# Up and down projections of the first layer in one program per engine

## The chip, the cores and the metric

The kernel runs on one core of a Trainium2 chip, in float32. The metric is the device time of one execution in microseconds (us): 2348.28 us is the median of three runs of the kernel before, which lie between 2337.39 and 2351.69 us. In the rows PE is TensorE's matmul side and PEld its weight loads, DVE is VectorE, ACT is ScalarE, POOL is GpSimd and SP is SyncE. A float32 matmul shows as two records in the trace.

## The reference

Two layers of a diffusion transformer act on 512 image tokens and, in the first layer, on 256 context tokens as well (width 1024). The change lies where the first layer's feed-forward part is computed and where the second layer begins:

```python
def conv_ffn(h, w_up, conv_w, w_down):            # d_ff = 2816
    a, g = jnp.split(dwconv(h @ w_up, conv_w), 2, axis=-1)   # depthwise, 3 taps over tokens
    return (jax.nn.silu(g) * a) @ w_down
...
        x = x + mx[:, :, 2] * rmsnorm(ox, norm_g[l, 1])
        hx = modulate(rmsnorm(x, norm_g[l, 2]), mx[:, :, 3], mx[:, :, 4])
        x = x + mx[:, :, 5] * rmsnorm(conv_ffn(hx, ffn_w_up[l], ffn_conv[l], ffn_w_down[l]), norm_g[l, 3])
        # the same for the context rows z in the first layer
...
    mx = (sc @ w_mod[l] + b_mod[l])               # of the next layer, l = 1
```

## The kernel before

The program is a row of stages. Each stage is a Block, in which every engine has its own list of instructions; at the end of a Block all engines meet before the next Block starts. The stages that matter here are `mix_and_up` (L1933: output projection of the mixer, then the up projection) and `down_and_project` (L2739: the down projection, then the second layer's input projections). Both are called from `layer_ab` (L3491, L3492). The second layer has the two in one Block already (`up_down_and_store`, L2963).

**Weights.** All weights come through a ring of four slots (`c.ring`). SP issues the loads in the order in which they are used; each waits until the products that read the slot's earlier content are done. In the up stage (`c.issue`, L182) the loads run up to four ahead of the stage's end, so the first four loads of the down projection (`down0x`) are issued there: two when the last column pair but one is done, two when the last is. The later ones are issued in the down stage (`c.stream`, L193): the two loads of part q wait for the products of part q-2.

**Up projection** (`mix_and_up_programs`, L1449). The 22 pairs of gate and value columns are numbered n = 0 to 21 (`FT` = 22). From n = 1 on, each pair is one Strassen step: seven products `p1, p2, p6, p5, p7, p3, p4`, each of four matmuls, on quarters of weights and tokens and on sums of quarters, which DVE makes (`join_weights(n)`, four additions, L1851 to L1856). The results are gathered from the banks by one ACT copy (L1708) and seven DVE additions (`add_up`, L1860, semaphore `whole`). In DVE's list pair n does this in order: `join_weights(n + 1)`, `convolve_pair(n - 1, 0)` and `convolve_pair(n - 1, 1)` (two taps each, L387 and L391), the additions of pair n, and among them `multiply(n - 1)` (L1829, semaphore `done`), after ACT's silu (L1678). After the last pair DVE calls `between()`, which does nothing in `mix_and_up`, then the convolutions of pair 21 and `multiply(21)`. The hidden rows, 22 tiles of 768 tokens, lie in the arena.

**Down projection** (`DownPairs`, L2367, and `FirstDownPairs`, L2514). The image rows are done in 8 steps, again of Strassen form. A step has three parts over the hidden rows k: `PARTS = ((0, 4), (4, 8), (8, 11))`; each part has the seven products in the order above, and the 21 products of a step accumulate in seven banks. DVE makes the sums of rows (`join_rows(group, part)`, L2562 to L2567) once for each group of four steps and the sums of weights (`join(q)`, L2429 to L2434) for each part. PE reads the weights for p1 and p2 as they are, waits for two sums before p6 and for four before p7. The third part reads hidden rows 8 to 10 and 19 to 21.

**Work beside it.** The second layer's modulation is computed in the down stage. POOL first issues five small loads of the filter network (`net.load`, L3564 to L3567; they go to `c.small`) and then the loads of `w_mod` (`load_side`, L2605, L2610), 512 KB each, two buffers in turn at the end of the arena. PE multiplies each loaded piece in its own list of instructions, between products of the down projection:

```python
    def behind_product(self, pe, s, n):                  # n: product 0 to 20 of step s
        if s < 4 and n % 5 == 0 and n:
            self.side_product(pe, 4 * s + n // 5 - 1)
    ...
    def side_product(self, pe, q):
        pe.wait_ge(self.mod_in[q % 2], 16 * (q // 2 + 1))   # piece q has landed
```

Products are counted through the parts, so n = 5 is p3 of part 0, n = 10 is p5 of part 1, n = 15 is p2 of part 2. ACT starts the down stage by issuing 24 small loads (L284, L295) and then keeps p1 of each step (`keep_first`, L2483).

`mix_and_up_programs` returns the lists of the engines and two waits, `gathered` (all additions of the up projection done) and `complete` (`done` at 22, so the last `multiply` is done).

Of the kernel before, what the change touches and what calls it, by code (L numbers as in the profile page):

```python
# [22 lines left out]
D = 1024  # L23
# [371 lines left out]
def outc(c):  # L395

    return c.arena[:, 0:KT * N_ALL].rearrange("p (k t) -> p k t", k=KT)
# [1051 lines left out]
def mix_and_up_programs(c, l, z, name, src, sem):  # L1449
# [261 lines left out]
        middle(FT - 1, 1)  # L1711
        gate(FT - 1)

    def vector(dve, between):
        v = nc.vector
        link = chain(dve, dve_chain)
        per = 2 if z else 1
# [177 lines left out]
        for n in range(begun, FT):  # L1895
            i = n - begun
            gate_rows, value_rows = ([fast.raw(n, half)[:, at:at + fast.half] for at in (0, fast.half)] for half in range(2))
            if n + 1 < FT:
                join_weights(n + 1)
            if i:  # L1900
                convolve_pair(n - 1, 0)
                convolve_pair(n - 1, 1)
            dve.wait_ge(copied, i + 1)
            add_up(i, gate_rows[1], gate_rows[0], "p6")
            add_up(i, gate_rows[0], gate_rows[0], "p2")
            multiply(n - 1)
            dve.wait_ge(whole, 7 * i + 1)
            add_up(i, value_rows[0], gate_rows[1], "p7")
            dve.wait_ge(whole, 7 * i + 3)
            add_up(i, value_rows[1], value_rows[0], "p5")  # L1910
            add_up(i, gate_rows[1], gate_rows[1], "p5")
            dve.wait_ge(whole, 7 * i + 5)
            add_up(i, gate_rows[1], gate_rows[1], "p3")
            add_up(i, value_rows[0], value_rows[0], "p4")
            join_hidden(n - 1)
# [12 lines left out]
            pe.wait_ge(hidden_joined, 4 * (FT // 2))  # L1928

    return sync, tensor, scalar, vector, gathered, complete  # L1930


def mix_and_up(c, l, z, name, src):  # L1933


    st, sem = stage(c)
    sync, tensor, scalar, vector, _, _ = mix_and_up_programs(c, l, z, name, src, sem)
    with st, c.nc.Block() as block:  # L1938
        @block.sync
        def _(sp):  # L1940
            sync(sp)

        @block.tensor
        def _(pe):
            tensor(pe)

        @block.scalar
        def _(act):
            scalar(act)

        @block.vector
        def _(dve):
            vector(dve, lambda: None)


class FastPairs:
# [557 lines left out]
class FirstDownPairs(DownPairs):  # L2514
# [8 lines left out]
    def __init__(self, c, sem, rows, side):  # L2523
        DownPairs.__init__(self, c, sem, rows)
        self.side, self.hidden = side, ffn_hidden(c)[0]
        self.mod_in = [sem("mod_in_even"), sem("mod_in_odd")]
        self.mod_used, self.mod_drained, self.rows_in, self.rows_joined, self.weighed = (
            sem(n) for n in ("mod_used", "mod_drained", "rows_in", "rows_joined", "mod_weighed"))
        late, gate, spare = c.ht[:, 4 * D:6 * D], c.gates[:, 0].rearrange("p u d -> p (u d)"), c.arena[:, FT * N_ALL:]
        whole = lambda ap: [ap[:, 128 * lo:128 * hi] for lo, hi in self.PARTS]  # L2530
        self.first_sums = (whole(late), whole(gate), [spare[:, 0:512], late[:, 1408:1920], gate[:, 1408:1792]])

    def weight_sums(self, q):
        slots = [(self.lo + 2 * q + h) % RING * SLOT + 1024 for h in range(2)]
# [201 lines left out]
                between(dve, n)  # L2736


def down_and_project(c):  # L2739

# [5 lines left out]
    spread = Spread(c, 1, sem)  # L2748
    pairs = FirstDownPairs(c, sem, rows, spread.m)
    down = Down(c, sem, rows, spread.m, pairs)  # L2750
    n_pairs, n_rope = 8, 2
    last_raw = c.ht[:, 4 * D:5 * D].rearrange("p (b t) -> p b t", b=2)
    row = lambda n: q[:, n, :] if n < 4 else u[:, n - 4, :]
# [11 lines left out]
    with st, nc.Block() as block:  # L2765
# [2 lines left out]

        @block.sync
        def _(sp):  # L2770
            for name in ("down0x", "down0", "swa_q", "hy_in", "swa_k", "swa_v"):
                c.stream(sp, name, 0 if name == "swa_v" else RING)

        @block.gpsimd
        def _(pool):
            net.load(pool)
            pairs.load_side(pool)

        @block.tensor
        def _(pe):  # L2780
            pe.wait_ge(c.tables_back, 32)
            for s in range(pairs.STEPS):
                pairs.step(pe, s)
            pe.wait_ge(pairs.copied, pairs.STEPS)
            pe.wait_ge(pairs.whole, 7 * pairs.STEPS)
            pe.wait_ge(pairs.mod_drained, 2)
# [48 lines left out]

        @block.scalar
        def _(act):
            spread.m.load_biases(act, pairs.rows_in)
            spread.m.load_gains(act, pairs.rows_in)
            for s in range(pairs.STEPS):  # L2840
                pairs.keep_first(act, s)
                pairs.square(act, s)

            def unit(n):
                if n % 2 == 0:
                    down.keep_act(act, n)
                if n:
                    down.square(act, n - 1)

            for q in range(n_units):  # L2850
                unit(q)
                if q == 1:
                    for i in range(TX):
                        rows.branch_root(act, i)
                if q in (3, 4):
                    for i in range(2 * (q - 3), 2 * (q - 3) + 2):
                        rows.norm_root(act, i)
                if 5 <= q < 5 + TX:
                    rows.modulate_act(act, q - 5, turn_banks)
            down.square(act, n_units - 1)  # L2860
            for i in range(TX, TT):
                rows.branch_root(act, i)
            rows.norm_root(act, TX)

            def others(act, i):
                if i == 0:
                    rows.norm_root(act, TX + 1)
                    rows.modulate_act(act, TX, late_banks)
                if i == 1:
                    rows.modulate_act(act, TX + 1, late_banks)  # L2870
                if i == 7:
                    net.sine(act, 0)
                if i in (4, 5):
                    act.wait_ge(rows.added, TT)
                    spread.keep_gate_act(act, i - 4, i - 4, 0, gate_banks)

            fast.scalar(act, others)
            net.sine(act, 1)
            swa_k.scalar(act)
            for t in range(0, TT, 2):  # L2880
                act.wait_ge(v_product, t + 1)
                nc.scalar.activation(v_[:, t, :], c.ps[:, (0, 2, 4, 5)[t % 4], 0:128], ACT.Copy).then_inc(v_act, 1)

        @block.vector
        def _(dve):
            dve.wait_ge(c.tables_back, 32)
            parts = pairs.n_parts
            for s in range(pairs.STEPS):
                group, first = s // pairs.PER_GROUP, s % pairs.PER_GROUP == 0
                if s == 0:  # L2890
                    pairs.join_rows(dve, 0, 0)
                    pairs.join(dve, 0)
                for part in range(1, parts):
                    if first:
                        pairs.join_rows(dve, group, part)
                    pairs.join(dve, parts * s + part)
                    if s >= 4:
                        pairs.weigh_behind(dve, s, part)
# [585 lines left out]
def layer_ab(c):  # L3484
# [3 lines left out]
    chunk_products(c)  # L3488
    delta_rule(c)
    gdn_output(c)  # L3490
    mix_and_up(c, 0, N_Z, "ab_out", outc(c))  # L3491
    down_and_project(c)  # L3492


def cd_buffers(c):
# [655 lines left out]
```

## Time and profile before

| | |
|---|---|
| median of three runs | 2348.28 us (2337.39 to 2351.69) |
| profiled execution, its time | 2345.86 us |
| profiled execution, its span from first to last instruction | 2344.1 us |
| PE busy | 2150.0 us, 92% of the span |
| DVE busy | 1497.9 us, 64% |
| mean granted clock of TensorE | 0.966 |
| up projection's last products, end | about 1218.0 us from the span's start |
| first product of the down projection | 1225.65 us |

In the timelines the first number is the start in us from the span's start, the second the length; "[idle before <-releaser]" is the engine's idle time ahead of the piece and what ended it. "xN" counts records. Pieces are merged, so a piece can hold short waits. In the table of stretches PEclk is the granted clock, 1.00 for 2.4 GHz and 0.50 for 1.2 GHz.

### The profile page before, as it was taken

What the parts mean: (1) busy time and instruction counts of PE and PEld (TensorE: products, weight loads), DVE (VectorE), ACT (ScalarE), POOL (GpSimd) and SP (SyncE); (2) the same over time, 40 slices, a digit from 0 to 9 for tenths busy, and PEclk for the clock granted to TensorE, in tenths of its full rate; (3) what the DMA queues carried; (4) which work ended last, traced back from release to release, by engine and by line L of the source; (5) the groups of instructions that cost most, each with busy time, mean ns of one, the idle gap of its engine ahead of it and who ended that gap; (6) DMA issues with size and microseconds to landing.
All of it is one profiled execution on the core that took longest, in us unless ns stands there. A gap on an engine that the chain in (4) does not pass through costs nothing. (4 is left out here: it accounts for less than half of the span.)

```text
span 2344.1 us, 38947 instructions
## 1 busy us (share of the span) xinstructions
PE 2150.0 (92%) x16226; PEld 1633.5 (70%) x16226; DVE 1497.9 (64%) x2822; ACT 539.1 (23%) x1187; POOL 248.8 (11%) x335
## 2 busy tenths in 40 slices
PE   5999989969997999999989989897888799999998
PEld 3566655558886755555558889785454588888998
DVE  4534856567775666665665656674676756778754
ACT  3103732431213421111110012111451032111111
POOL 2000100037760000000000111000210000000000
PEclk8999989989999999999999999998898899999999
DMA  8450002100004112122217678332000213323454
GB/s 311 146 196 19 1 19 54 36 2 4 4 4 145 37 53 55 54 54 67 59 56 245 219 221 247 112 90 68 1 1 19 72 37 90 86 80 87 141 167 143
DMA packets 235633, 205.09 MB, mean 87 GB/s; under 512 B 6771, under 2 KB 219458, under 8 KB 235266
## 3 DMA queue, kind: packets, MB, share of 16 engines
q1 hardware_dynamic: 222050, 157.07, 22.6%
q0 software_dynamic: 12416, 42.32, 5.4%
q10 hardware_dynamic: 992, 3.21, 0.4%
q8 instruction: 129, 2.11, 0.4%
q14 instruction: 46, 0.38, 0.1%
HBM read 200.48 MB, written 2.10 MB: 86 GB/s over the span
## 5 line engine op out<-in xcount | busy, mean ns | idle before, releaser
L1599 PE MATMUL banks<-mem 128*128 128x384 f32 (+1 forms) x2296 | 622.1, 433 | 0.0
L1599 PEld LDWEIGHTS banks<-mem 128*128 128x128 f32 x2296 | 434.4, 189 | 187.2
L2453 PE MATMUL banks<-mem 128*128 128x128 f32 x2464 | 285.5, 277 | 18.1 <-PEq L1938 7.7
L2453 PEld LDWEIGHTS banks<-mem 128*128 128x128 f32 x2464 | 279.3, 192 | 29.5 <-issue 23.5
L2013 PE MATMUL banks<-mem 128*128 128x256 f32 (+1 forms) x672 | 180.0, 424 | 9.4 <-ACT mem L3385 5.1
L2013 PEld LDWEIGHTS banks<-mem 128*128 128x128 f32 x672 | 128.4, 193 | 60.7 <-issue 21.3
L1860 DVE TENSOR_TENSOR mem<-mem,banks 128x384 f32<-128x384 f32 (+1 forms) x287 | 131.1, 487 | 39.4 <-PE banks L1599 36.7
L694 PE MATMUL banks<-mem 128*128 128x384 f32 x448 | 146.4, 485 | 2.1 <-PEq L440 1.4
L996 PE MATMUL banks<-mem 64*64 64x64 f32 x3840 | 127.7, 220 | 18.5 <-DVE mem L1272 11.4
L996 PEld LDWEIGHTS banks<-mem 64*64 64x64 f32 x3840 | 120.1, 136 | 28.7 <-DVE mem L1272 13.7
L1524 PE MATMUL banks<-mem 128*128 128x256 f32 x560 | 127.2, 388 | 11.0 <-PEq L1388 8.8
L1524 PEld LDWEIGHTS banks<-mem 128*128 128x128 f32 x560 | 108.5, 195 | 28.0 <-issue 11.8
L1851 DVE TENSOR_TENSOR mem<-mem 128x512 f32<-128x512 f32 x41 | 28.4, 694 | 154.4 <-DMA mem<-in_ffn_w_up 154.4
L694 PEld LDWEIGHTS banks<-mem 128*128 128x128 f32 x448 | 84.6, 189 | 60.5 <-issue 1.6
L1678 ACT ACTIVATE mem<-mem 128x768 f32<-128x768 f32 (+1 forms) x44 | 32.5, 739 | 346.5 <-DVE mem L391 346.5
L391 DVE SCALAR_TENSOR_TENSOR mem<-mem 128x511 f32<-128x511 f32 (+1 forms) x160 | 100.9, 659 | 3.8
L387 DVE SCALAR_TENSOR_TENSOR mem<-mem 128x511 f32<-128x511 f32 (+1 forms) x160 | 100.6, 658 | 1.2 <-ACT mem L2054 1.1
L1687 ACT ACTIVATE mem<-mem 128x768 f32<-128x768 f32 (+1 forms) x82 | 66.1, 829 | 146.5 <-DVE mem L1860 146.3
L2340 PE MATMUL banks<-mem 128*128 128x128 f32 x704 | 82.5, 278 | 2.6 <-DVE mem L2186 2.4
L2340 PEld LDWEIGHTS banks<-mem 128*128 128x128 f32 x704 | 81.0, 195 | 4.6 <-DVE mem L2186 2.5
L2094 DVE TENSOR_TENSOR mem<-mem,banks 128x256 f32<-128x256 f32 (+1 forms) x84 | 36.9, 465 | 56.1 <-PE banks L2013 55.6
L2429 DVE TENSOR_TENSOR mem<-mem 128x512 f32<-128x512 f32 (+3 forms) x40 | 29.8, 745 | 58.7 <-DMA mem<-in_ffn_w_down 58.5
(401 smaller groups left out, 2964.9 us busy)
## 6 DMA issues: line engine op xcount, KB each, us to landing
mem<-in_ffn_w_up SPq DMA_DIRECT2D x88, 512.0 KB, 5.1
mem<-in_w_mod POOLq DMA_DIRECT2D x48, 512.0 KB, 5.0
mem<-in_w_mod POOLq DMA_DIRECT2D x16, 1024.0 KB, 7.3
mem<-in_ffn_w_down SPq DMA_DIRECT2D x32, 512.0 KB, 4.7
mem<-in_ab_w_in SPq DMA_DIRECT2D x24, 512.0 KB, 5.2
mem<-in_ffn_w_down SPq DMA_DIRECT2D x16, 768.0 KB, 6.1
mem<-in_ffn_w_down SPq DMA_DIRECT2D x16, 704.0 KB, 6.6
mem<-in_ffn_w_down SPq DMA_DIRECT2D x16, 640.0 KB, 5.4
```

Source lines behind the costliest of these rows:

```text
L387: step = v.scalar_tensor_tensor(out[:, 1:n], src[:, 0:n - 1], tap(0), out[:, 1:n], ALU.mult, ALU.add)
L391: step = v.scalar_tensor_tensor(out[:, 0:n - 1], src[:, 1:n], tap(2), out[:, 0:n - 1], ALU.mult, ALU.add)
L694: last = nc.tensor.matmul(fast.out(i, name), weights[:, k, :], tokens[:, k, :], start=k == 0, stop=k == 3)
L996: last = mm(c.ps[pa, LEVEL[i], fr], lhs[pa, fr], rhs[pa, fr], start=True, stop=True)
L1524: last = nc.tensor.matmul(mixed_out(s, name), rows[:, k, :], columns[:, k, :], start=k == 0, stop=k == 3)
L1599: last = nc.tensor.matmul(fast.out(i, name), weights[:, k, :], tokens[:, k, :], start=k == 0, stop=k == 3)
L1687: f(dst[:, 0:n_all], fast.raw(n, half), ACT.Identity, scale=middle_tap(n, half)).then_inc(drained, 1)
L1860: v.tensor_tensor(to, one, fast.out(i, name), ALU.add).then_inc(whole, 1)
L2013: last = self.c.nc.tensor.matmul(self.out(i, name), weights[:, k, :], tokens[:, k, :], start=k == 0, stop=k == 3)
L2094: self.c.nc.vector.tensor_tensor(to, one, self.out(i, name), ALU.add).then_inc(self.whole, 1)
L2340: last = c.nc.tensor.matmul(c.ps[:, n % self.BANKS, 0:128], hidden[:, k, t * 128:(t + 1) * 128], w, start=k == 0, stop=k == FT - 1)
L2453: last = c.nc.tensor.matmul(self.out(name), rows(k), weights[:, k - lo, :], start=k == 0, stop=k == 10)
```

## The change

`mix_and_up` and `down_and_project` become one stage, `up_down_and_project`, with one list per engine: first the engine's part of the up projection, then its part of the down projection, with no meeting of the engines between them. DVE makes the weight sums of part 0 (`join(0)`) in the place where, in the last pair, there is no next pair to join; between the last additions and the last two convolutions it makes the row sums of parts 0 and 1 and the weight sums of part 1. PE waits for `gathered` and begins with the down products; it waits for `complete` before part 2. POOL, ACT and DVE wait for `complete` before their work of the down stage. One of the places that hold row sums moves from the arena to `c.ht`.

```diff
-    def vector(dve, between):
+    def vector(dve, between, last=lambda: None):
...
             if n + 1 < FT:
                 join_weights(n + 1)
+            else:
+                last()
             if i:
                 convolve_pair(n - 1, 0)
                 convolve_pair(n - 1, 1)
...
-        late, gate, spare = c.ht[:, 4 * D:6 * D], c.gates[:, 0].rearrange("p u d -> p (u d)"), c.arena[:, FT * N_ALL:]
+        late, gate, second = c.ht[:, 4 * D:6 * D], c.gates[:, 0].rearrange("p u d -> p (u d)"), c.ht[:, 2 * D:4 * D]
...
-        self.first_sums = (whole(late), whole(gate), [spare[:, 0:512], late[:, 1408:1920], gate[:, 1408:1792]])
+        self.first_sums = (whole(late), whole(gate), [second[:, 0:512], late[:, 1408:1920], gate[:, 1408:1792]])
...
-def down_and_project(c):
+def up_down_and_project(c):
...
+    up_sync, up_tensor, up_scalar, up_vector, gathered, complete = mix_and_up_programs(c, 0, N_Z, "ab_out", outc(c),
+                                                                                         lambda name: sem(f"up_{name}"))
...
         @block.sync
         def _(sp):
+            up_sync(sp)
             for name in ("down0x", "down0", "swa_q", "hy_in", "swa_k", "swa_v"):
                 c.stream(sp, name, 0 if name == "swa_v" else RING)
...
         @block.gpsimd
         def _(pool):
+            complete(pool)
             net.load(pool)
             pairs.load_side(pool)
...
         @block.tensor
         def _(pe):
+            up_tensor(pe)
+            gathered(pe)
             pe.wait_ge(c.tables_back, 32)
             for s in range(pairs.STEPS):
-                pairs.step(pe, s)
+                pairs.step(pe, s, complete)
...
         @block.scalar
         def _(act):
+            up_scalar(act)
+            complete(act)
             spread.m.load_biases(act, pairs.rows_in)
...
         @block.vector
         def _(dve):
-            dve.wait_ge(c.tables_back, 32)
+            def early_parts():
+                dve.wait_ge(c.tables_back, 32)
+                pairs.join_rows(dve, 0, 0)
+                pairs.join(dve, 1)
+                pairs.join_rows(dve, 0, 1)
+
+            up_vector(dve, early_parts, lambda: pairs.join(dve, 0))
+            complete(dve)
             parts = pairs.n_parts
             for s in range(pairs.STEPS):
                 group, first = s // pairs.PER_GROUP, s % pairs.PER_GROUP == 0
-                if s == 0:
-                    pairs.join_rows(dve, 0, 0)
-                    pairs.join(dve, 0)
-                for part in range(1, parts):
+                for part in range(1 if s else 2, parts):
...
-    mix_and_up(c, 0, N_Z, "ab_out", outc(c))
-    down_and_project(c)
+    up_down_and_project(c)
```

## Rows read from the trace of the kernel before

**Rows 1.** The page, busy time by engine: busy us (share of the span) xinstructions.
```profile
PE 2150.0 (92%) x16226; PEld 1633.5 (70%) x16226; DVE 1497.9 (64%) x2822; ACT 539.1 (23%) x1187; POOL 248.8 (11%) x335
```

**Rows 2.** Timeline of PE, 1100 to 1420 us.
```profile
1099.62 118.33 PE L1599 MATMUL banks<-mem 128*128 128x384 f32 x366
1225.65 7.70 PE L2453 MATMUL banks<-mem 128*128 128x128 f32 x48 [7.71 <-PEq L1938]
1233.29 0.61 PE L316 MATMUL banks<-mem 128*2 128x256 f32 x8
1233.83 4.73 PE L2453 MATMUL banks<-mem 128*128 128x128 f32 x40
1238.49 0.61 PE L316 MATMUL banks<-mem 128*2 128x256 f32 x8
...
1243.25 0.61 PE L316 MATMUL banks<-mem 128*2 128x256 f32 x8
```

**Rows 3.** Timeline of DVE, 1217 to 1232 us.
```profile
1217.99 0.56 DVE L1860 TENSOR_TENSOR mem<-mem,banks 128x384 f32<-128x384 f32 x1 [1.96 <-PE banks L1599]
1218.46 1.14 DVE L387 SCALAR_TENSOR_TENSOR mem<-mem 128x511 f32<-128x511 f32 x2
...
1223.93 0.96 DVE L1829 TENSOR_TENSOR mem<-mem 128x768 f32<-128x768 f32 x1 [0.91 <-ACT mem L1678]
1225.51 0.69 DVE L2562 TENSOR_TENSOR mem<-mem 128x512 f32<-128x512 f32 x1 [0.61 <-PEq L1938]
...
1228.05 0.69 DVE L2429 TENSOR_TENSOR mem<-mem 128x512 f32<-128x512 f32 x1
...
1230.58 0.69 DVE L2562 TENSOR_TENSOR mem<-mem 128x512 f32<-128x512 f32 x1
```

**Rows 4.** DMAs of the down weights issued 1217 to 1219 us; min/median/max.
```profile
L182 SPq DMA_DIRECT2D mem<-in_ffn_w_down x2: 367/437/507, 1218.0 to 1218.4; - x2
...
DMA to landing us min/median/max: 3.5/4.0/4.5
```

**Rows 5.** Timeline of POOL, 1100 to 1420 us.
```profile
1225.94 0.60 POOL L3564 DMA_DIRECT2D mem<-in_hy_w  x1 [516.40 <-POOLq L1938]
...
1229.14 1.11 POOL L2610 DMA_DIRECT2D mem<-in_w_mod  x2
1234.23 0.53 POOL L2610 DMA_DIRECT2D mem<-in_w_mod  x1 [3.97 <-PE banks L316]
```

**Rows 6.** DMAs of w_mod, 1150 to 1300 us; min/median/max.
```profile
L2610 POOL DMA_DIRECT2D mem<-in_w_mod x15: 528/528/583, 1229.1 to 1296.0; - x15
...
DMA to landing us min/median/max: 4.0/4.7/6.7
```

**Rows 7.** Stretches around the boundary: us, busy (x) by engine, PEclk, DMA share, GB/s.
```profile
1218.00:1225.60 7.60, 0.00 (x0) 0.00 (x0) 6.00 (x11) 1.78 (x2) 0.00 (x0) 0.79 0.41 138
1225.60:1228.00 2.40, 2.35 (x11) 2.38 (x12) 2.37 (x4) 0.00 (x0) 2.06 (x4) 0.50 0.06 16
1228.00:1229.50 1.50, 1.37 (x7) 1.11 (x6) 1.47 (x4) 0.00 (x0) 1.50 (x4) 0.60 0.08 10
1229.50:1233.30 3.80, 3.78 (x34) 3.66 (x37) 3.77 (x7) 0.00 (x0) 0.76 (x2) 1.00 0.72 240
```

**Rows 8.** Another restart of PE after an idle stretch: timeline, 715 to 742 us.
```profile
731.94 10.43 PE L1524 MATMUL banks<-mem 128*128 128x256 f32 x34 [8.75 <-PEq L1388]
```

**Rows 9.** The stretch of that restart, columns as in rows 7.
```profile
728.00:738.00 10.00, 6.06 (x15) 4.84 (x16) 9.54 (x12) 2.46 (x4) 0.00 (x0) 0.52 1.05 396
```

**Rows 10.** The second layer's boundary between up and down, 2180 to 2220 us.
```profile
2192.38 0.42 DVE L1860 TENSOR_TENSOR mem<-mem,banks 128x256 f32<-128x256 f32 x1 [1.24 <-PE banks L1599]
...
2192.86 2.94 PE L2453 MATMUL banks<-mem 128*128 128x128 f32 x24 [0.51 <-DVE mem L1860]
```

**Rows 11.** Timeline of ACT, 1196 to 1250 us.
```profile
1231.69 5.01 ACTq L295 DMA_DIRECT2D mem<-in_norm_g  x16
1242.69 0.28 ACT L2483 ACTIVATE mem<-banks 128x128 f32<-128x128 f32 x1 [18.79 <-PE banks L2453]
```

More of the change, by code:

```diff
@@ L1930, in mix_and_up_programs @@
     return sync, tensor, scalar, vector, gathered, complete
[L1933 to L1953, printed above, removed]
 class FastPairs:
```

## The prediction

> **What bounds the kernel now.** I read the page first. PE is busy for 92% of the span [rows 1], so what counts is whether an edit shortens or lengthens the time in which PE stands still. Then I read PE's own timeline around the place of the change. The last up products run without a gap until 1099.62 + 118.33 = 1217.95 us; then PE stands still for 7.71 us, released by the meeting of the engines, and the first down product starts at 1225.65 us [rows 2]. DVE's timeline tells what fills this gap: the last addition ends at 1217.99 + 0.56 = 1218.55, then come the convolutions of pair 21 from 1218.46, the wait for the silu and the last multiply, which ends at 1223.93 + 0.96 = 1224.89 [rows 3]. The clock table tells that the gap costs more than its length: the granted clock falls in it and is 0.50, that is 1.2 GHz, when PE restarts; it is back at 2.4 GHz only from about 1229.3 on [rows 7]. Last I read POOL's timeline, because PE's list holds modulation products behind down products: PE's first one stands at 1233.29 [rows 2], and the load that it needs was issued at 1229.14 [rows 5].
>
> So the most there is to win here is the gap of 7.7 us and a little around it, 0.4% of the whole.
>
> **The change part by part.**
>
> *The start of the down products.* PE needs `gathered`, the end of the last addition, 1218.55. In the second layer, where the two stages are one already, PE starts 2192.86 - (2192.38 + 0.42) = 0.06 us after that addition [rows 10]. So p1 of part 0 starts at 1218.6 instead of 1225.65: 7.0 us earlier. Its weight sums are ready long before: they are made in the place of a `join_weights`, in the last pair's time, in which DVE waited for PE anyway (1.96 us of idle time before the last addition alone [rows 3]). I cost `join(0)` at nothing. If that cover were gone, it would cost up to its own length, four instructions in 1230.58 - 1228.05 = 2.53 us [rows 3].
>
> *Part 0 up to its sixth product.* DVE starts `join_rows(0, 0)` where the convolutions started, at 1218.46; four such instructions take 1228.05 - 1225.51 = 2.54 us [rows 3], so two sums are there at 1219.7 and four at 1221.0. A record of the down products takes 4.73 / 40 = 0.118 us at the full clock [rows 2], a product of part 0 (eight records) 0.95 us. p1 and p2 end at 1220.5, p6 and p5 at 1222.4, p7 and p3 at 1218.6 + 48 x 0.118 = 1224.3. The clock is still full then, because PE hardly paused.
>
> *What stands behind p3.* After product n = 5, p3 of part 0, PE's list holds the first modulation product, which waits for the first piece of `w_mod`. Its load is the sixth DMA in POOL's list, and POOL now begins with `complete`. PE takes its list in order, so p4 of part 0 and all that follows stand behind this wait, and so does the load of part 2's weights, which waits for p4. This decides the time, so I work out when `complete` comes.
>
> *When DVE completes.* DVE's list after the last addition is now: `join_rows(0, 0)`, done at 1221.0; `join(1)`, which waits for weights whose loads are issued when pair 21 is done, the second at 1218.4, landed 4.5 us later, at 1222.9 [rows 4]: a wait of 1.9 us with the last convolutions queued behind it; its four sums, 2.53 us, to 1225.4; `join_rows(0, 1)`, 2.54 us, to 1228.0; then the convolutions, silu and multiply, which took 1224.89 - 1218.46 = 6.43 us [rows 3], to 1234.4. Before, that point was 1224.89: `complete` comes 9.5 us later, because 7.6 us of sums and 1.9 us of waiting were put ahead of it.
>
> *When the first piece lands.* POOL follows an event of another engine by 0.33 us: PE's first modulation product ends at 1233.29 + 0.61 = 1233.90, POOL goes on at 1234.23 [rows 2, 5]. So POOL starts at 1234.7 (before, with the meeting of the engines, 1225.94). From its first small load to the first of `w_mod` it needs 1229.14 - 1225.94 = 3.20 us [rows 5]: issue at 1237.9. Landing takes 4.0 us at least, 4.7 in the median and 6.7 at most [rows 6]. For the first piece it can't have been more than 1233.29 - 1229.14 = 4.15 us, since PE used it then. I take 4.1 us: 1242.0. The bounds are 4.0 and 6.7.
>
> The Trainium skill ("DMA: Bandwidth & Descriptors", section on the anatomy of one DMA on the GpSimd path) fits such a DMA as 2.0 us and its bytes over 436 GB/s, an estimate of 3.2 us for 512 KB. The rows have 4.0 as the least, so the measurement decides; by the page the sum would be 0.9 us less.
>
> So PE stands still from 1224.3 to 1242.0, 17.7 us, where it stood still for 7.7 us before, and passes this point of its list at 1242.0 instead of 1233.29: **8.7 us later**.
>
> *The clock at the second restart.* Before, PE restarted at 1225.65 and had the full clock from about 1229.3 (0.60 in 1228 to 1229.5, 1.00 after [rows 7]), some 3.7 us at half speed. That cost nothing, because p6 waited for sums until 1229.4 in any case (two of `join(0)`, half of 2.53 us after 1228.05 [rows 3]). After the change the slow stretch falls on work that waits for nothing: the modulation product, p4 and part 1, whose sums are ready since 1228. Half of 3.7 us is 1.85 us. From below this cost is 0, if the clock should still be full. From above: another restart, at 731.94 after 8.75 us of idle time [rows 8], lies in a stretch of 728 to 738 with a mean of 0.52 [rows 9], so the full clock came some 0.4 us before its end, 5.7 us after the restart; half of that is 2.85 us. I take 1.9 us, this place's own row.
>
> *What follows.* The modulation pieces after the first are loaded as PE uses them, and part 2's weights are loaded behind p4, so both shift with PE. ACT's 24 small loads are issued after `complete`. Before, they ended at 1231.69 + 5.01 = 1236.7, and p1 of the step was kept at 1242.69 [rows 11], so there were 6 us of room; both now move by about 10 us, and the room stays. Part 2's row sums start at 1234.4, long before PE is there. The meeting of the engines that is gone is in the numbers above (POOL's 1.05 us between 1224.89 and 1225.94 becomes 0.33). I find nothing later that starts by itself and could take the delay up; after 1233.29 PE runs on its own products [rows 2].
>
> **The sum.** 8.7 + 1.9 = 10.6 us more. On the profiled execution's time of 2345.86 us (span 2344.1 and 1.8 around it) this gives 2356.5 us. That execution is 2.4 us below the median of the three runs, 2348.28; counted from the median it would be 2358.9. I keep 2356.5 us.
>
> **The rivals.**
>
> *A: nothing holds PE, and the kernel is faster.* If the first piece had landed by the time PE passes p3 (1224.3), PE would go on: its modulation product 0.6 and p4 0.95, to 1225.9; p1 and p2 of part 1 to 1227.7, the rest of the part with its modulation product to 1233.0; then `complete` at 1234.4, p1 and p2 of part 2 (12 records) and a product of modulation; the weight sums follow DVE's row sums (four short ones, some 1.9 us, and two of the next four, 0.9 us) at about 1237.2. Before, p6 of part 2 stood at 1243.25 + 0.6 = 1243.8 [rows 2], so 6.6 us are won: 2339.3 us. For it speaks that PE's gap is real and that the second layer has no such gap [rows 10]. Against it: the piece would have to be issued by 1224.3 - 4.0 = 1220.3, and POOL's list has `complete` first, which can't be before 1224.89 even if DVE did no sums. Chance 0.05.
>
> *B: the pieces land late.* At 6.7 us instead of 4.1 [rows 6] it is 2.6 us more, and with the clock's upper bound 1.0 more: 2360.1 us, and 2362.5 counted from the median. For it: the pieces travel beside ACT's small loads, as before. Against it: the down weights no longer travel then, since those of part 2 wait for p4. Chance 0.09.
>
> *C: the clock stays low after the long pause.* At 1.2 GHz a down record takes 2.35 / 11 = 0.214 us [rows 7], 0.096 more than at the full clock. If PE kept that clock through steps 0 and 1 (two times 77 matmuls, two records each, less the 48 records done before the pause: 260), it would lose 25 us in place of 1.9: 2345.86 + 8.7 + 25 = 2379.6 us, slower by 1.4%. It passes 1% from a loss of 14.8 us on, that is when 154 records, a whole step, run slow. Against it: at both restarts in the rows the full clock was back in less than 6 us of work [rows 7 to 9]. Chance 0.03. The Trainium skill ("TensorE: Matmul & The Clock Gate", SECTION) says that the clock has been seen stuck low for over 50 us; no row here shows that.
>
> *D: the change doesn't do what it says*, because `join(0)` waits long for its weights, the convolutions of pair 20 come late and the last additions with them. Against it: DVE's idle time in the last pair. It would add a few us to the forecast, 2359 us. Chance 0.03.
>
> **How the numbers follow.** The forecast has a chance of 0.80. Its own bounds are 0.1 us less and 2.6 more for the landing, 1.9 less and 1.0 more for the clock: 2354.5 to 2360.1, or up to 2362.5 from the median. Runs of the kernel before spread over 14 us, 8 below and 6 above the profiled one, and the kernel after will do the same. So I give 2346 to 2366 us; left out are A, C and the ends of this spread. About 1% is what a measurement of this kernel can tell from no change; that is 23 us. The forecast, A, B and D lie within it, 0.97 together; C lies above. Of the 0.97 I leave 0.02 on the faster and 0.01 on the slower side for what I overlook. So: faster 0.02, within 1% 0.94, slower 0.04.
>
> **What would show it.** Right: PE's first down product some 0.1 us after the last addition, PE idle between p3 of part 0 and the first modulation product for 16 to 20 us, with a DMA of `w_mod` as the releaser; POOL's first load some 9 us later than before; the last multiply after 1233; a granted clock of 0.5 at PE's second restart. Wrong: the first modulation product before 1236, POOL's loads before the last multiply, or a PE that runs from part 0 into part 1 without a gap.

## The result and the profile after

The changed kernel takes 2363.86 us (median of eight runs, 2356.07 to 2367.71), the kernel before 2349.35 us (median of eight). The ratio is 1.0063 with an interval of [1.0047, 1.0078], that is 14.8 us more (11.0 to 18.3), within the 1% that the prediction called no change. The forecast was 2356.5 us, and 10.6 us more.

The page of the changed kernel: the span, then the busy time by engine in the form of [rows 1].

```profile
span 2365.4 us, 38937 instructions
...
PE 2163.8 (91%) x16226; PEld 1641.7 (69%) x16226; DVE 1499.8 (63%) x2822; ACT 539.8 (23%) x1187; POOL 249.4 (11%) x335
```

No instruction of an engine's work was added, yet the span is longer. PE's timeline shows the place, which answers to [rows 2] (the down products are at L2432 here, L316 are the modulation products):

```profile
1218.07 5.62 PE L2432 MATMUL banks<-mem 128*128 128x128 f32 x48 [0.65 <-DVE mem L1860]
1242.06 1.03 PE L316 MATMUL banks<-mem 128*2 128x256 f32 x8 [18.36 <-DMA mem<-in_w_mod]
1243.03 6.00 PE L2432 MATMUL banks<-mem 128*128 128x128 f32 x40
1248.96 0.61 PE L316 MATMUL banks<-mem 128*2 128x256 f32 x8
1249.50 4.29 PE L2432 MATMUL banks<-mem 128*128 128x128 f32 x36
```

Counted from the start of the last addition, the down products begin 7.0 us earlier than before (0.61 us behind it instead of 7.66), and do 48 records without a pause, six products of part 0. Then PE waits 18.36 us for a DMA of `w_mod`. The old gap of 7.71 us is gone and a gap of 18.36 us stands a little behind it. Read the releaser in the brackets: it is neither DVE nor the down weights.

DVE's timeline, answering to [rows 3], shows what comes between the last addition and the last multiply (L2541 begins a group of row sums, L2408 one of weight sums):

```profile
1217.46 0.56 DVE L1860 TENSOR_TENSOR mem<-mem,banks 128x384 f32<-128x384 f32 x1 [1.96 <-PE banks L1599]
1217.93 0.69 DVE L2541 TENSOR_TENSOR mem<-mem 128x512 f32<-128x512 f32 x1
...
1222.46 0.69 DVE L2408 TENSOR_TENSOR mem<-mem 128x512 f32<-128x512 f32 x1 [1.91 <-DMA mem<-in_ffn_w_down]
...
1225.01 0.69 DVE L2541 TENSOR_TENSOR mem<-mem 128x512 f32<-128x512 f32 x1
...
1227.54 1.14 DVE L387 SCALAR_TENSOR_TENSOR mem<-mem 128x511 f32<-128x511 f32 x2
...
1233.01 0.96 DVE L1829 TENSOR_TENSOR mem<-mem 128x768 f32<-128x768 f32 x1 [0.91 <-ACT mem L1678]
```

The convolutions (L387) start at 1227.54 instead of right after the addition, so the last multiply ends at 1233.97. POOL's list, answering to [rows 5], starts 0.3 us behind that:

```profile
1234.27 0.60 POOL L3554 DMA_DIRECT2D mem<-in_hy_w  x1 [525.26 <-DVE mem L1829]
...
1237.55 1.08 POOL L2589 DMA_DIRECT2D mem<-in_w_mod  x2
```

and PE uses the first piece 4.51 us after its issue. The table of stretches, columns as in [rows 7], has the clock at the second restart:

```profile
1230.00:1242.00 12.00, 0.00 (x0) 0.00 (x0) 5.08 (x9) 0.84 (x1) 4.34 (x8) 0.50 0.28 89
1242.00:1245.50 3.50, 3.44 (x19) 2.59 (x20) 0.00 (x0) 0.00 (x0) 0.53 (x1) 0.50 0.29 73
1245.50:1249.00 3.50, 3.50 (x35) 3.38 (x37) 0.00 (x0) 0.00 (x0) 0.00 (x0) 0.97 0.78 263
```

At a granted clock of 0.50 PE does 19 records in 3.5 us, eight of them those of the modulation product; at 0.97 it does 35.

### The profile page after: what moved, and what is told of

Same layout as the page of the kernel before. It is cut to its first block and busy times, and to the rows that moved or that the text cites. A ratio compares the mean times of both kernels' runs of the same rounds, so it can differ in the third digit from the quotient of the medians.

```text
span 2365.4 us, 38937 instructions
## 1 busy us (share of the span) xinstructions
PE 2163.8 (91%) x16226; PEld 1641.7 (69%) x16226; DVE 1499.8 (63%) x2822; ACT 539.8 (23%) x1187; POOL 249.4 (11%) x335
## 3 DMA queue, kind: packets, MB, share of 16 engines
q8 instruction: 129, 2.11, 0.4%
## 5 line engine op out<-in xcount | busy, mean ns | idle before, releaser
L2432 PEld LDWEIGHTS banks<-mem 128*128 128x128 f32 x2464 | 278.7, 192 | 21.1 <-issue 14.4
L2432 PE MATMUL banks<-mem 128*128 128x128 f32 x2464 | 284.1, 276 | 10.0 <-issue 3.9
L1860 DVE TENSOR_TENSOR mem<-mem,banks 128x384 f32<-128x384 f32 (+1 forms) x287 | 131.0, 487 | 33.0 <-PE banks L1599 30.2
L387 DVE SCALAR_TENSOR_TENSOR mem<-mem 128x511 f32<-128x511 f32 (+1 forms) x160 | 100.5, 656 | 1.2 <-ACT mem L2033 1.1
L2408 DVE TENSOR_TENSOR mem<-mem 128x512 f32<-128x512 f32 (+3 forms) x40 | 29.8, 745 | 76.7 <-DMA mem<-in_ffn_w_down 76.5
```

What stands on the lines that cost most here:

```text
L387: step = v.scalar_tensor_tensor(out[:, 1:n], src[:, 0:n - 1], tap(0), out[:, 1:n], ALU.mult, ALU.add)
L1860: v.tensor_tensor(to, one, fast.out(i, name), ALU.add).then_inc(whole, 1)
L2432: last = c.nc.tensor.matmul(self.out(name), rows(k), weights[:, k - lo, :], start=k == 0, stop=k == 10)
```

## The experiments

Every execution reaches this place at a slightly different time. To compare the traces I count from the start of the last addition (the last L1860, in two kernels L1864) to the first modulation product (L316) and to the thirteenth, in step 3. Times are starts in us; the shift is the distance from the last addition to the thirteenth, less the 77.12 us of the kernel before (1295.11 - 1217.99). The thirteenth, in the kernel before and in the changed one:

```profile
1295.11 0.61 PE L316 MATMUL banks<-mem 128*2 128x256 f32 x8
```

```profile
1305.57 0.61 PE L316 MATMUL banks<-mem 128*2 128x256 f32 x8
```

| kernel | last addition | first L316 | thirteenth L316 | shift | ratio to before |
|---|---|---|---|---|---|
| before | 1217.99 | 1233.29 | 1295.11 | 0 | 1 |
| after | 1217.46 | 1242.06 | 1305.57 | +11.0 | 1.0063 [1.0047, 1.0078] |
| after_again | 1216.05 | 1240.20 | 1305.60 | +12.4 | 1.0066 [1.0047, 1.0086] |
| sums_after | 1215.82 | 1230.96 | 1292.48 | -0.5 | 1.0003 [0.9981, 1.0025] |
| held | 1217.02 | 1239.96 | 1304.53 | +10.4 | 1.0049 [1.0033, 1.0065] |
| small_last | 1216.39 | 1237.72 | 1303.81 | +10.3 | one run |
| kept_busy | 1216.70 | 1241.10 | 1304.18 | +10.4 | one run |
| kept_busy_2 | 1215.40 | 1239.70 | 1302.76 | +10.2 | one run |
| pieces_early | 1215.30 | 1221.46 | 1298.86 | +6.4 | 1.0013 [0.9998, 1.0029] |
| act_free | 1217.44 | 1223.61 | 1296.86 | +2.3 | 1.0000 [0.9984, 1.0017] |
| all_moved | 1215.07 | 1221.24 | 1286.57 | -5.6 | 0.9972 [0.9958, 0.9987] |

The shift is that of one execution, the ratio that of many. Behind the thirteenth product the profiled executions take between 1046.0 us (sums_after) and 1059.8 us (after) to their end, and all_moved, the furthest ahead at the thirteenth, takes 1058.0. So a shift is not to be read as the time won or lost within a few us.

**sums_after: are the early sums the price?** The three groups of sums between the last additions and the last convolutions go back behind `complete`.

```diff
             def early_parts():
                 dve.wait_ge(c.tables_back, 32)
-                pairs.join_rows(dve, 0, 0)
-                pairs.join(dve, 1)
-                pairs.join_rows(dve, 0, 1)
...
-                for part in range(1 if s else 2, parts):
+                if s == 0:
+                    pairs.join_rows(dve, 0, 0)
+                for part in range(1, parts):
```

> The changed kernel with no sums between the last additions and the last convolutions: row sums of parts 0 and 1 and the weight sums of part 1 are made after complete, as before the change. Theory (the first modulation piece holds PE, and its load waits for complete, which the early sums put off): the last multiply ends some 9.5 us earlier than in the changed kernel, near 1224.5, POOL starts near 1224.8, the first modulation product stands near 1232.5 instead of 1242.06, and the time is 9 to 10 us below the changed kernel's, a ratio to the kernel before of 0.999 to 1.001. Rival 1 (one list per engine costs by itself, for instance by the lost meeting of the engines): the ratio stays at 1.005 to 1.007. Rival 2 (the early sums are worth their place, PE waits longer without them): slower than the changed kernel.

The first modulation product stands 15.1 us after the last addition (24.6 in the changed kernel, 15.3 before), and the ratio is 1.0003. So one list per engine costs nothing by itself that these runs could tell (the interval reaches 0.25% up and 0.19% down), and it brings nothing here either: the loss comes from what was put ahead of the last convolutions. PE's timeline shows that it now waits for the row sums (L2543) and not for the piece:

```profile
1216.43 2.05 PE L2432 MATMUL banks<-mem 128*128 128x128 f32 x16 [0.65 <-DVE mem L1860]
1224.33 6.70 PE L2432 MATMUL banks<-mem 128*128 128x128 f32 x32 [5.84 <-DVE mem L2543]
1230.96 0.61 PE L316 MATMUL banks<-mem 128*2 128x256 f32 x8
```

**held: does a late piece alone cost as much, without the change?** The kernel before, with POOL held up ahead of the first piece.

```diff
             net.load(pool)
+            for i in range(12):
+                at = 2 * D + 512 + 64 * i
+                pool.dma_start(c.ht[0:2, at:at + 64], a["hy_freq"][0, 0:2, :]).then_inc(held, 16)
+            pool.wait_ge(held, 16 * 12)
             pairs.load_side(pool)
```

> The kernel before the change, two stages and no early sums, with twelve small loads more and a wait for them in POOL's list ahead of the first modulation piece, which puts that piece off by 8 to 8.5 us. Theory (the time is set by when the first piece lands, and the earlier start of the down products is worth nothing while PE waits for it): first modulation product some 23.5 us after the last addition's end, as in the changed kernel (24.0), against 14.7 before; a shift of 8 to 10.5 us, ratio 1.0035 to 1.0065. Rival (the merged lists cost by themselves, beside the late piece): clearly below the changed kernel, ratio 1.002 or less.

```profile
1224.68 3.70 PE L2453 MATMUL banks<-mem 128*128 128x128 f32 x16 [7.70 <-PEq L1938]
1228.54 3.84 PE L2453 MATMUL banks<-mem 128*128 128x128 f32 x32 [0.16 <-DVE mem L2431]
1239.96 1.04 PE L316 MATMUL banks<-mem 128*2 128x256 f32 x8 [7.58 <-DMA mem<-in_w_mod]
```

Here PE has both gaps, 7.70 us at the meeting of the engines and 7.58 us for the piece. The first modulation product stands 22.9 us after the last addition, the shift is 10.4 us and the ratio 1.0049. Counted from the last addition, the down products start 7.0 us later than in the changed kernel (7.66 against 0.61), and the shift is the same within a us: when the piece lands sets the time, and the earlier start counts for nothing. The first product itself comes 1.7 us sooner than in the changed kernel, and 0.8 of that goes in the slow stretch behind it: the first two modulation products stand 7.68 us apart here, 6.90 there.

**small_last: the 3.2 us of small loads.** POOL issues the first two pieces, then the network's loads.

```diff
         for q in range(self.BOTH):
+            if q == 2:
+                small(pool)
             if q >= 2:
                 pool.wait_ge(self.mod_used, q - 1)
...
             complete(pool)
-            net.load(pool)
-            pairs.load_side(pool)
+            pairs.load_side(pool, net.load)
```

> The changed kernel with POOL's five small loads of the filter network behind the first two pieces of w_mod instead of ahead of them. Theory: POOL's list up to the first piece is 3.2 us shorter, so the first modulation product stands near 1238.8 instead of 1242.06, and everything after it, the end too, comes 3.2 us earlier than in the changed kernel. Rival (PE's wait is set by something else than the first piece's issue, for instance by the part's sums or the down weights): the product stays at 1242 within 0.5 us.

The product moved as expected, to 21.3 us after the last addition, 3.3 us sooner. The second half missed: at the thirteenth product only 0.7 us is left of it (+10.3 against +11.0). In steps 1 to 3 PE waited 3.5 us in all, 0.7 of it for the down weights by name and 2.8 put down to "issue". This is one execution of each. The changed kernel had 1.2 us of such waits in its first profiled execution and 2.5 in after_again, without any change; so what a us saved here is worth by step 3 is not settled.

**kept_busy and kept_busy_2: is the slow restart the clock's?** 64 and then 80 matmuls are put into PE's wait; their results are overwritten.

```diff
     def side_product(self, pe, q):
+        if q == 0:
+            for i in range(80):
+                self.c.nc.tensor.matmul(self.c.ps[:, 7, 0:128], self.c.tab["ident"], self.c.tab["ones"], start=True, stop=True)
```

> The changed kernel with 64 matmuls of table constants into the modulation's own bank ahead of the first modulation product (their results are overwritten), so that PE works some 15 us of its 18 us wait. Theory (1.6 to 1.9 us of the loss are the low clock at the second restart): the first modulation product stays at 1242.0, the granted clock there is 1.00 in place of 0.50, and the second product stands 5.2 us after the first instead of 6.9; the shift against the kernel before is 1.6 us smaller from there on. Rival (the slow stretch after the pause is not the clock's): the distance of the two stays near 6.9 us.

> As kept_busy with 80 matmuls in place of 64, since 64 left a pause of 3.9 us in which the clock fell after all. They end some 0.5 us before the first piece lands. Theory (clock): granted clock 1.00 through the first two modulation products, which stand 5.2 us apart (6.9 in the changed kernel, 6.8 in kept_busy). Rival (the slow stretch comes from the loads that land then, not from the clock): 6.8 us again.

With 64 matmuls a pause of 3.87 us was left, the clock was down again just as PE restarted (0.59 in 1241 to 1244 us, the first row below), and the two products stood 6.79 us apart: a miss that told nothing. With 80 the pause was 0.20 us and the clock stayed up (the second row, and PE's timeline):

```profile
1241.00:1244.00 3.00, 2.90 (x19) 2.43 (x20) 0.00 (x0) 0.00 (x0) 0.53 (x1) 0.59 0.40 108
```

```profile
1241.00:1244.00 3.00, 3.00 (x29) 3.00 (x28) 0.00 (x0) 0.00 (x0) 0.17 (x1) 1.00 0.70 160
```

```profile
1221.47 18.03 PE L2568 MATMUL banks<-mem 128*128 128x128 f32 x160
1239.70 0.61 PE L316 MATMUL banks<-mem 128*2 128x256 f32 x8 [0.20 <-DMA mem<-in_w_mod]
1240.24 4.73 PE L2432 MATMUL banks<-mem 128*128 128x128 f32 x40
1244.90 0.61 PE L316 MATMUL banks<-mem 128*2 128x256 f32 x8
```

The products stand 5.20 us apart, as before the change [rows 2], and the granted clock of 1241 to 1244 us is 1.00. So the 1.7 us (6.90 - 5.20) at the second restart are the clock's. Counted from the last addition, the second modulation product comes 2.0 us sooner than in the changed kernel (29.5 against 31.5). By the thirteenth 0.8 of that is left: PE had 2.5 us of waits in steps 1 to 3, where the changed kernel had 1.2. The 1.6 us that kept_busy expected from there on were not kept.

**pieces_early: rival A made true.** The first eight pieces go to a place that the up projection has left when its last product is done, so POOL needn't wait for `complete` with them.

```diff
+    def piece(self, q):
+        o = (FT + 3) * N_ALL + D * (q % 2)
+        return self.c.arena[:, o:o + D] if q < 8 else self.weights[:, q % 2, :]
...
         for q in range(self.BOTH):
+            if q == 8:
+                small(pool)
...
-            complete(pool)
-            net.load(pool)
-            pairs.load_side(pool)
+            multiplied(pool)
+
+            def small(pool):
+                complete(pool)
+                net.load(pool)
+
+            pairs.load_side(pool, small)
```

(`multiplied` is a wait for the last up product.)

> The changed kernel with the first eight modulation pieces in a place of the arena that the up projection has left when its last product is done, so that POOL begins with them there and does complete and its small loads ahead of the ninth piece. Theory (the wait for the first piece is the whole loss; without it the early start is worth what rival A of the prediction works out): the first modulation product stands before 1225, PE next waits for complete near 1234 ahead of part 2, p6 of part 2 stands near 1237 (1243.8 before, 1254.3 in the changed kernel), and the time is 17 us below the changed kernel's, 6 to 7 below the kernel before: a ratio of 0.997. Rival (the pieces and the down weights then get in each other's way, or the early sums hold PE at part 2 as well): p6 of part 2 after 1243, ratio of 1.000 or above.

Half right. The wait for the piece is gone, the first product stands 6.2 us after the last addition, and the ratio fell from 1.0063 to 1.0013. But the forecast for this kernel was 0.997, and PE's timeline shows four waits in step 0 and behind it in the place of one:

```profile
1227.34 2.02 PE L2439 MATMUL banks<-mem 128*128 128x128 f32 x16 [2.04 <-DVE mem L2550]
...
1234.89 1.58 PE L2439 MATMUL banks<-mem 128*128 128x128 f32 x12 [2.11 <-DVE mem L1833]
1236.40 0.61 PE L316 MATMUL banks<-mem 128*2 128x256 f32 x8
1237.99 3.61 PE L2439 MATMUL banks<-mem 128*128 128x128 f32 x30 [0.98 <-DVE mem L2417]
1241.54 0.61 PE L316 MATMUL banks<-mem 128*2 128x256 f32 x8
1246.55 7.22 PE L2439 MATMUL banks<-mem 128*128 128x128 f32 x48 [4.39 <-ACT mem L2469]
```

Part 1 waits 2.04 us for its row sums (L2550), part 2 waits 2.11 us for `complete` and 0.98 us for its weight sums (L2417), and step 1 waits 4.39 us for ACT. Behind this last wait the 48 records take 7.22 us instead of the 5.62 of step 0; the granted clock of 1246.5 to 1250 us is 0.57. ACT's timeline says why PE waits for it:

```profile
1234.78 6.17 ACTq L284 DMA_DIRECT2D mem<-in_b_mod  x8
1240.99 5.09 ACTq L295 DMA_DIRECT2D mem<-in_norm_g  x16
1246.12 0.28 ACT L2469 ACTIVATE mem<-banks 128x128 f32<-128x128 f32 x1 [12.37 <-issue]
```

ACT issues its 24 loads for 11.3 us and keeps p1 only then; the additions of step 0, and so the banks of step 1, stand behind that. The 6 us of room that the prediction found here [rows 11] were room only as long as PE was late itself. The first wait, 2.04 us for part 1's row sums, has a cause in the DMAs: DVE's list makes these sums behind the weight sums of part 1, whose weights landed late. These are the down weights issued as the up projection ends, in the same form as [rows 4]:

```profile
L182 SPq DMA_DIRECT2D mem<-in_ffn_w_down x2: 367/437/507, 1215.3 to 1215.7; - x2
...
DMA to landing us min/median/max: 3.5/5.5/7.4
```

The second landed after 7.4 us instead of 4.5, with the two pieces from POOL's queue now on the way too. So it is in every trace: 7.4, 7.9 and 7.7 us in the three kernels with early pieces (pieces_early, act_free, all_moved), 4.4 to 4.7 us in the other eight. The Trainium skill ("DMA: Bandwidth & Descriptors", section "Issuing engines are not separate DMA queues") says that the DMAs of all issuing engines run on the same 16 DMA engines and interleave; the 7.4 us agree with it.

**act_free: the small loads out of ACT's way.** As pieces_early, and:

```diff
             up_sync(sp)
+            spread.m.load_biases(sp, pairs.rows_in)
...
-            spread.m.load_biases(act, pairs.rows_in)
-            spread.m.load_gains(act, pairs.rows_in)
             for s in range(pairs.STEPS):
                 pairs.keep_first(act, s)
                 pairs.square(act, s)
+                if s == 0:
+                    spread.m.load_gains(act, pairs.rows_in)
```

> As pieces_early, and the 24 small loads that ACT issues after complete (11.3 us in which it can't keep p1 of step 0) are moved: eight to SP behind its last loads of the up stage, sixteen on ACT behind step 0's squares. Theory (in pieces_early ACT's loads took the place of the wait that was removed: PE idle 4.4 us for keep_first, and a second low stretch of the clock): no wait of PE for ACT after step 0, step 1 begins within 1 us of step 0's last modulation product instead of 4.4, and the time is 5 to 6 us below pieces_early, a ratio to the kernel before of 0.998 to 1.000. Rival (the small loads only move the wait: drain in step 1 or the down weights of part 2 hold PE as long): the ratio stays at 1.001.

PE's wait for ACT is gone, step 1 follows at once, and the shift falls by 4.1 us, from +6.4 to +2.3. The ratio of 1.0000 is at the upper end of what was expected, 0.0013 or some 3 us below pieces_early where 5 to 6 were forecast. A low stretch of the clock came here too, behind the waits of 2.04 and 2.11 us that are left: the granted clock of 1239 to 1245 us is 0.50, and the 30 records from p6 of part 2 on take 6.05 us instead of 3.61:

```profile
1240.56 6.05 PE L2439 MATMUL banks<-mem 128*128 128x128 f32 x30 [0.53 <-DVE mem L2417]
```

**all_moved: DVE's order as well.** As act_free, and the row sums of parts 0 and 1 come first, the weight sums of part 1 between the last two convolutions.

```diff
-        between()
+        between(0)
         convolve_pair(FT - 1, 0)
+        between(1)
         convolve_pair(FT - 1, 1)
...
-            def early_parts():
-                dve.wait_ge(c.tables_back, 32)
-                pairs.join_rows(dve, 0, 0)
-                pairs.join(dve, 1)
-                pairs.join_rows(dve, 0, 1)
+            def early_parts(place):
+                if place == 0:
+                    dve.wait_ge(c.tables_back, 32)
+                    pairs.join_rows(dve, 0, 0)
+                    pairs.join_rows(dve, 0, 1)
+                else:
+                    pairs.join(dve, 1)
```

> As act_free, and DVE makes the row sums of parts 0 and 1 first, then one pair of the last convolutions, then the weight sums of part 1 (whose weights now land 7.4 us after issue, beside the two modulation pieces), then the other pair. Theory: complete comes some 13 us after the last addition instead of 19, PE's waits for part 1's row sums (2.0 us) and for complete (2.1 us) nearly go, p6 of part 2 stands near 17.5 us after the last addition's end (25.3 before, 22.1 in pieces_early), and the time is 4 to 5 us below act_free, a ratio of 0.996 to 0.998. Rival (the wait moves to part 2's weights): p6 of part 2 not earlier than in act_free.

```profile
1215.68 5.62 PE L2440 MATMUL banks<-mem 128*128 128x128 f32 x48 [0.65 <-DVE mem L1864]
1221.24 0.61 PE L316 MATMUL banks<-mem 128*2 128x256 f32 x8
1221.78 1.16 PE L2440 MATMUL banks<-mem 128*128 128x128 f32 x8
1223.33 3.81 PE L2440 MATMUL banks<-mem 128*128 128x128 f32 x32 [0.39 <-DMA mem<-in_ffn_w_down]
1227.07 0.61 PE L316 MATMUL banks<-mem 128*2 128x256 f32 x8
1227.62 4.29 PE L2440 MATMUL banks<-mem 128*128 128x128 f32 x36
1231.83 0.61 PE L316 MATMUL banks<-mem 128*2 128x256 f32 x8
1233.27 3.62 PE L2440 MATMUL banks<-mem 128*128 128x128 f32 x30 [0.83 <-DVE mem L2418]
```

Step 0 runs almost without a pause: p6 of part 2 stands at 1233.27, 17.6 us after the last addition's end, the largest wait of step 0 is 0.83 us, and the granted clock is 1.00 throughout, from 1215 to 1262 us. The ratio is 0.9972 [0.9958, 0.9987], 6.6 us below the kernel before: this version beats both kernels. Counted from the start of the last addition, p6 of part 2 comes at 18.2 us, 7.6 sooner than before (25.8); 2 of the 7.6 us are gone by step 3, after waits such as 1.39 us for the down weights of step 1.

**after_again: the changed kernel a second time.**

> The changed kernel itself once more, unaltered. The first measurement gave a ratio of 1.0063 [1.0047, 1.0078], 11.0 to 18.3 us, where the trace's stretch around the change accounts for 10.6. Theory (the rest is the scatter of the later stages, where the low stretches of the clock fall differently in every execution): a ratio near 1.0045, 10 to 11 us, and a first modulation product again some 24.0 us after the last addition's end. Rival (a delay here costs some 4 us more in the later stages every time): 1.006 to 1.007 again.

The ratio is 1.0066, so the loss is near 15 us and not near 10.6, and the theory's 1.0045 was a miss. The stretch up to step 3 accounts for 11.0 and 12.4 us in the two profiled executions; what lies behind, some 3 to 4 us, is within the interval's width but on the same side twice. The two executions of this one kernel, 2365.4 and 2355.8 us long, differ most behind 1660 us: the same product (L3659) stands at 1663.34 us in the one and 1662.79 in the other, the first of L3969 at 1790.72 and 1782.08. This is that stretch in the first and then in the second:

```profile
1660.00:1700.00 40.00, 36.19 (x167) 21.11 (x166) 24.92 (x65) 16.03 (x38) 9.74 (x8) 0.72 0.00 1
```

```profile
1660.00:1700.00 40.00, 36.00 (x215) 21.04 (x213) 29.58 (x80) 19.34 (x47) 9.97 (x8) 0.90 0.00 1
```

PE is busy for the same 36 us but does 167 records or 215, at a clock of 0.72 or 0.90. Nothing there was changed. Of the 9.6 us between these two executions, 8.1 arise between the two places. Whether a delay in the down stage makes such slow stretches more frequent, which would explain the 3 to 4 us, stays open. No run here separates that from chance, and pieces_early and act_free give a fixed price no support: by their ratios they lose 3.0 and 0.0 us, less than their shifts of 6.4 and 2.3.

## Why the prediction was right

**The place and the cause: right.** PE starts early, runs to p3 of part 0 and stands behind the first modulation product, released by a DMA of `w_mod`. sums_after takes the delay of `complete` away and the loss goes; held puts the piece off in the kernel before and a loss of the same size comes.

**The chain to the piece: right step by step.** Counted from the start of the last addition, forecast against the changed kernel: first down product 0.6 against 0.61; weights of part 1 landed 4.9 against 5.0; last multiply done 16.4 against 16.5; POOL's start 16.7 against 16.8; first piece issued 19.9 against 20.1; first modulation product 24.0 against 24.6. The largest miss is the landing: 4.1 us were taken, and the piece was used 4.51 us after its issue (3.88 in after_again). Each term came from a row of the kernel before, because only the order of known pieces changed.

**The clock: right in kind, a little small or large by where one looks.** 1.9 us were forecast; the two first modulation products stand 6.90 us apart in the changed kernel and 5.20 in the kernel before, so 1.7 us (2.0 in after_again, where they stand 7.18 us apart), and kept_busy_2 shows that it is the clock. The clock was back some 3.5 us after the restart, and rival C did not come. The sentence of the Trainium skill that stands beside rival C is from "TensorE: Matmul & The Clock Gate", section "Seeing it yourself"; it belongs to a warning there against trusting the clock's records in traces, and no run here shows such a stretch.

**The sum: too small.** Forecast 8.7 + 1.9 = 10.6. Up to the second modulation product the two terms measured 9.3 + 1.7 in the first profiled execution and 8.9 + 2.0 in after_again; the stretch to step 3 gave 11.0 and 12.4, the measurement 14.8. The step that fell short is "What follows", where nothing later was found to add to the delay. Up to step 3 that held in the first execution (1.2 us of waits in steps 1 to 3, against 1.0 in the kernel before) and not in after_again (2.5 us); behind it lie the unsettled 3 to 4 us.

**The time: in the range, in part by luck.** The forecast of 2356.5 us missed 2363.86 by 7.4. Of these, 3.9 are the sum (the medians differ by 14.5 us) and 3.5 the base: the prediction counted from the profiled execution's 2345.86, and the median of the kernel before is 2349.35. The bounds that it worked out for its own terms end at 2360.1, or at 2362.5 from the median, and the measured time lies above both. It is within 2346 to 2366 because the scatter of single executions was added to the range, not because a term foresaw it.

**Rival A: right that it couldn't come, wrong in its price.** It took 6.6 us as won if nothing held PE for the piece. pieces_early lost 1.0013 - 1 of the time, some 3 us, with that wait gone. The price left out that ACT's 24 loads then stand ahead of `keep_first` (4.39 us) and that pieces and down weights, on the way together, land later (7.4 instead of 4.5 us, so 2.04 us for the row sums, and the last multiply done 19.4 us after the start of the last addition where A had 16.4). all_moved, with ACT's loads moved and DVE's sums in another order, has 6.6 us as well, but the equal number is a coincidence: A assumed the old order of the sums, and all_moved won 7.6 us at p6 of part 2, where A had 6.6, and lost part of it again behind.

**Rivals B and D.** The piece was used 4.51 us after issue, not 6.7. DVE's last additions were not late: the same 1.96 us of idle time stands ahead of the last one in both kernels.

## What to carry to other kernels

When two stages are merged, look in the bottleneck engine's list for the first instruction that waits for something which could start only after the old boundary, and work out when that now starts; an engine that begins earlier only to stand behind such an instruction has won nothing. Work pulled ahead of the last step of the earlier stage puts off everything that waits for this step, on every engine and queue. And when a wait is removed, price the next ones by their own lists: here ACT's loads, with 6 us of room before, became the next wait as soon as PE was on time.

## What the runs showed that was not expected

The clock fell over a pause of 3.87 us of PE (kept_busy, where the granted clock of 1241 to 1244 us was 0.59) and did not over one of 0.20 us (kept_busy_2, 1.00). And time saved early in the down stage partly came back as waits in steps 1 to 3 (by the thirteenth product small_last kept 0.7 of 3.3 us, kept_busy_2 0.8 of 2.0), so a us in step 0 was not a us at the end in these single executions.
